# Score matmuls in three fp32r passes over the two row halves, two query tiles started a position ahead, and GpSimd's work of a position tied to VectorE's scalings

## What is computed

```python
q, k, v = split_heads(h, w_qkv, N_HEADS, HEAD_DIM)
q = apply_rope(q, cos, sin) * (HEAD_DIM ** -0.5)
k = apply_rope(k, cos, sin)
oa = moba_attention(q[:, :MOBA_HEADS], k[:, :MOBA_HEADS], v[:, :MOBA_HEADS])
ob = dilated_attention(q[:, MOBA_HEADS:], k[:, MOBA_HEADS:], v[:, MOBA_HEADS:])
o = jnp.concatenate([oa, ob], axis=1)
return merge_heads(o) @ w_o
```

## Time and profile before

| | |
|---|---|
| median of 3 runs (lowest, highest) | 1213.09 us (1212.98, 1213.19) |
| the profiled execution's own time | 1213.26 us |
| its span, first to last instruction | 1211.5 us |
| PE / PEld busy | 1188.8 us (98%) / 1049.2 us (87%) |
| DVE / ACT / POOL busy | 723.8 us (60%) / 628.0 us (52%) / 681.8 us (56%) |
| layer 0's positions 0 to 7 | 75.62 to 234.17 us of the span, 158.55 us |
| PE busy in positions 0 to 5 | all of it |

### The profile page before, as it was taken

One profiled execution on the slowest core, in us unless ns is written; L12 is line 12 of the kernel. 1 busy time (PEld: TensorE's weight loads), 2 busy tenths in 40 slices (PEclk: granted clock), 3 DMA queues, 4 the chain that ended last, 5 costly groups with the idle time before them and its releaser, 6 DMA issues.

```text
span 1211.5 us, 20288 instructions
## 1 busy us (share of the span) xinstructions
PE 1188.8 (98%) x7714; PEld 1049.2 (87%) x7714; DVE 723.8 (60%) x1368; ACT 628.0 (52%) x1089; POOL 681.8 (56%) x418
## 2 busy tenths in 40 slices
PE   9999999899999999999999999999999999999996
PEld 9877777689999999888888788878999999998885
DVE  2045656449988888612280356553999888872126
ACT  3145646446766666622342467663666666662223
POOL 4543535157877777655534332335587777765453
PEclk9999999999999999999999999999999999999999
DMA  7321121221232222432222121112022223233211
GB/s 283 125 72 73 67 85 70 71 105 36 105 112 106 104 106 103 133 130 77 102 105 107 69 71 69 70 70 104 36 106 104 104 104 104 104 133 110 104 69 70
DMA packets 20041, 117.44 MB, mean 97 GB/s; under 512 B 2448, under 2 KB 2832, under 8 KB 7568
## 3 DMA queue, kind: packets, MB, share of 16 engines
q1 hardware_dynamic: 18400, 112.21, 25.8%
q10 hardware_dynamic: 1584, 4.51, 1.1%
HBM read 110.41 MB, written 2.10 MB: 93 GB/s over the span
## 4 chain that ended last, share of the span: by engine, by line
PE 85%; DVE 8%; ACT 2%; POOL 2%; issue 2%; DVEq 0%; ACTq 0%
PE bank L1491 33%; PE bank L1192 29%; PE bank L1223 14%; POOL w_lo L302 2%; PE bank L1275 2%; PE bank L1302 1%; PE bank L1361 1%; PE bank L1340 1%; PE bank L1289 1%; ACT w_hi L403 1%; DVE ln_mul L810 1%; DVE x L833 1%; PE bank L1350 1%; PE bank L1167 1%; DVE x L790 1%
## 5 line engine op out<-in xcount | busy, mean ns | idle before, releaser
L302 POOL TENSOR_TENSOR w_lo<-w_raw,w_hi 128x1024 fp32r<-128x1024 f32 x116 | 299.1, 2600 | 364.4 <-ACT w_hi L403 353.9
L403 ACT ACTIVATE w_hi<-w_raw 128x2048 fp32r<-128x2048 f32 x55 | 105.2, 1912 | 206.1 <-PE bank L1192 197.5
L1491 PE MATMUL bank<-t_hi,w_hi 128*128 128x256 f32 x640 | 181.3, 283 | 2.6 <-DVE w_lo L1046 2.6
L1491 PE MATMUL bank<-t_hi,w_lo 128*128 128x256 f32 x640 | 181.1, 283 | 0.0
L1491 PE MATMUL bank<-t_lo,w_hi 128*128 128x256 f32 x640 | 181.1, 283 | 0.0
L361 POOL TENSOR_TENSOR w_lo<-w_raw,w_hi 128x512 fp32r<-128x512 f32 x120 | 156.1, 1302 | 20.4 <-ACT w_hi L615 19.5
L1192 PE MATMUL bank<-w_hi,a_hi 128*128 128x512 f32 x480 | 153.4, 395 | 3.2 <-POOL w_lo L302 1.8
L1192 PE MATMUL bank<-w_hi,a_lo 128*128 128x512 f32 x480 | 152.0, 391 | 0.0
L1192 PE MATMUL bank<-w_lo,a_hi 128*128 128x512 f32 x480 | 151.8, 391 | 0.0
L1223 PE MATMUL bank<-xt_hi,w_hi 128*128 128x512 f32 (+1 forms) x416 | 147.1, 354 | 2.4 <-ACT v_all L433 1.7
L1223 PE MATMUL bank<-xt_lo,w_hi 128*128 128x512 f32 (+1 forms) x416 | 147.8, 355 | 0.0
(11 more groups left out here) (130 smaller groups left out, 2508.2 us busy)
## 6 DMA issues: line engine op xcount, KB each, us to landing
w_raw<-w_stream SPq DMA_DIRECT2D x97, 1024.0 KB, 4.8
x<-x_in SPq DMA_DIRECT2D x4, 512.0 KB, 7.5
gain<-ln_in ACTq DMA_DIRECT2D x4, 512.0 KB, 5.8
shift<-ln_in ACTq DMA_DIRECT2D x4, 512.0 KB, 7.1
qs<-qc SPq DMA_DIRECT2D x16, 128.0 KB, 2.0
ks<-kc SPq DMA_DIRECT2D x16, 128.0 KB, 2.0
out<-x SPq DMA_DIRECT2D x3, 512.0 KB, 2.6
w_raw<-w_stream SPq DMA_DIRECT2D x2, 512.0 KB, 6.4
```

Source lines behind the costliest of these rows:

```text
L302: pool.tensor_tensor(w_lo[slot(c)][:, part], w_raw[s][:, part], w_hi[slot(c)][:, part].bitcast(F32), ALU.subtract).then_inc(lo_ready, 1)
L403: act.activation(w_hi[slot(c)][:, :], w_raw[c % 2][:, :], ACT.Copy).then_inc(hi_ready, 2)
L1491: mm = pe.matmul(out, lhs[s][:, at], rhs[:, k, :], start=(k, v) == (0, 0), stop=(k, v) == (3, 2))
```

## The change

The scores are computed from split operands. The rotated q and k go to `qa_raw` and `ka_raw`; ScalarE makes their fp32r high parts (`q_heads`, `k_heads`), GpSimd the low part of q (`q_rest`), VectorE that of k (`k_rest`). `scores` then issues for a tile three passes, each with one matmul per head over all its keys (128, 256, 384 or 512 columns). Tiles 0 and 1 lie side by side in a bank, and their scores are issued at the end of the position before; their transposes go together, as do the weighings of tiles 0 and 1 and those of tiles 2 and 3, each value block meeting both query tiles in one matmul. Four places to fill are left of six.

On GpSimd the two units of a chunk's rest are taken apart. The work of a position is in this order: after VectorE's scaling of tile 1 (`p_ok`) the second unit of one chunk and the first product of q; after that of tile 2 the rest of q's rotation, the values' copy and `q_rest`; after `k_ok` the first unit of the next chunk. On ScalarE the weights' heads run one chunk earlier and behind the copy of k; q is copied for two positions ahead at the end of a position. The gain and shift of the first layer norm are loaded after position 7 instead of at the start, since `qa_raw` and `ka_raw` lie in their place.

```diff
-            def rest(c, it=0):
+            def rest(c, it=0, units=(0, 1)):
                 s = c % 2
-                for u in range(2):
+                for u in units:
 
                     pool.wait_ge(hi_ready, 2 * (whole(c) + 2 * it) + u + 1)
                     part = slice(u * UNIT, (u + 1) * UNIT)
                     pool.tensor_tensor(w_lo[slot(c)][:, part], w_raw[s][:, part],
                                        w_hi[slot(c)][:, part].bitcast(F32), ALU.subtract).then_inc(lo_ready, 1)
...
+            def q_cos(i):
 
                 a = A[0]
                 pool.wait_ge(a["q_sw"], 32 * (i + 1))
-                for n, (t, tab) in enumerate(((qc, 0), (qs, 1))):
-                    pool.tensor_tensor(t[:, :], t[:, :], rope[:, tab, :], ALU.mult).then_inc(a["q_m"], 1)
-                pool.wait_ge(a["q_m"], 2 * i + 2)
-                pool.tensor_tensor(qa[slot][:, :], qc[:, :], qs[:, :], ALU.add).then_inc(a["q_ok"], 1)
-                pool.wait_ge(a["q_ok"], i + 1)
+                pool.tensor_tensor(qc[:, :], qc[:, :], rope[:, 0, :], ALU.mult).then_inc(a["q_m"], 1)
+
+            def q_sum(slot, i):
+
+                a = A[0]
+                pool.tensor_tensor(qs[:, :], qs[:, :], rope[:, 1, :], ALU.mult).then_inc(a["q_m"], 1)
+                pool.wait_ge(a["q_m"], 4 * i + 2)
+                pool.tensor_tensor(qa_raw[slot][:, :], qc[:, :], qs[:, :], ALU.add).then_inc(a["q_m"], 1)
+
+            def q_rest(slot, i):
+
+                a = A[0]
+                pool.wait_ge(a["q_m"], 4 * i + 4)
+                pool.tensor_tensor(qa_lo[slot][:, :], qa_raw[slot][:, :], qa_hi[slot][:, :].bitcast(F32),
+                                   ALU.subtract).then_inc(a["q_ok"], 1)
...
+                def even_position(j, it=0):
+
+                    a, i = A[0], 2 * it + j
+                    n, after = (j + 1) % 2, i + 1
+                    pool.wait_ge(a["p_ok"], 4 * i + 2)
+                    rest(b + AT_QK + 2 + j, it, (1,))
+                    q_cos(after)
+                    pool.wait_ge(a["p_ok"], 4 * i + 3)
+                    q_sum(n, after)
+                    take_values(j + 1, it)
+                    q_rest(n, after)
+                    pool.wait_ge(a["k_ok"], after + 1)
+                    rest(b + AT_QK + 3 + j, it, (0,))
...
+            def query_copied(i):
+                a = A[0]
+                act.wait_ge(a["q_mm"], i + 1)
+                act.activation(qc[:, :], bank[0][:, :], ACT.Copy, scale=-MOBA_SCALE).then_inc(a["q_cp"], 1)
+
+            def q_heads(s, i):
+                a = A[0]
+                act.wait_ge(a["q_m"], 4 * i + 3)
+                act.activation(qa_hi[s][:, :], qa_raw[s][:, :], ACT.Copy).then_inc(a["q_m"], 1)
+
+            def k_heads(s, i):
+                a = A[0]
+                act.wait_ge(a["k_m"], 4 * i + 3)
+                act.activation(ka_hi[s][:, :], ka_raw[s][:, :], ACT.Copy).then_inc(a["k_m"], 1)
...
+                exps(0)
+                exps(1)
+                divide(0)
+                divide(1)
+                if before:
+                    out_heads(a, i - 1, (c - 1) % 2)
+                turned(0)
+                exps(2)
+                divide(2)
+                if dense:
+                    act.wait_ge(w_used, b + AT_QK + i + 2)
+                    act.activation(kc[:, :], bank[1][:, :], ACT.Copy).then_inc(a["k_cp"], 1)
+                    heads(b + AT_QK + c + 3, it)
+                exps(3)
+                turned(1)
+                divide(3)
+                if dense:
+                    q_heads((c + 1) % 2, i + 1)
+                turned(2)
+                if dense:
+                    k_heads((c + 1) % 2, i + 1)
+                if early:
+                    query_copied(i + 2)
...
+            def k_rest(a, s, i):
+
+                dve.wait_ge(a["k_m"], 4 * i + 4)
+                dve.tensor_tensor(ka_lo[s][:, :], ka_raw[s][:, :], ka_hi[s][:, :].bitcast(F32),
+                                  ALU.subtract).then_inc(a["k_ok"], 1)
...
+                bounds(0)
+                bounds(1)
+                divide(0)
+                divide(1)
+                turned(0)
+                bounds(2)
+                divide(2)
+                if before:
+                    out_rests(a, i - 1, (c - 1) % 2)
+                turned(1)
+                bounds(3)
                 if dense:
                     rope_k_cos(a, (c + 1) % 2, i + 1)
+                divide(3)
+                if dense:
                     rope_k_sin(a, (c + 1) % 2, i + 1)
-                turn_out(a, NT - 1, 0, 4, 4 * i + NT - 1)
+                turned(2)
+                if dense:
...
-                share = (8, 8, 9, 9, 9, 3) if early else (8, 8, 8, 3, 3) if dense else (3, 5, 7, 7, 6)
+                share = (15, 13, 13, 7) if early else (15, 9, 3, 3) if dense else (9, 9, 7, 5)
...
+                def scores(*tiles, p=par):
+
+                    for qi in tiles:
+                        at, L = P if qi == 1 else 0, (qi + 1) * P
+                        for n, (q, k) in enumerate(((qa_hi, ka_hi), (qa_hi, ka_lo), (qa_lo, ka_hi))):
+                            for h in range(2):
+                                part = slice(64 * h, 64 * h + 64)
+                                mm = pe.matmul(bank[2 + h][:, at:at + L], q[p][part, qi * P:(qi + 1) * P],
+                                               k[p][part, 0:L], start=n == 0, stop=n == 2)
+                    mm.then_inc(a["s_mm"], 1)
...
+                def weigh(*tiles):
+
+                    if tiles[0] == 0:
+                        pe.wait_ge(a["v_pos"], i + 1)
+                    pe.wait_ge(a["tev_v"], 3 * i + max(tiles[-1], 1))
+                    pe.wait_ge(a["tev_a"], 3 * i + max(tiles[-1], 1))
+                    for k in range(tiles[-1] + 1):
+                        q = slice(max(k, tiles[0]) * P, (tiles[-1] + 1) * P)
...
+                            mm = pe.matmul(bank[6 + par][part, q], v_pos[par][:, k, part], probs_t[h][:, k, q],
+                                           start=k == 0, stop=k == tiles[-1])
+                    if tiles[-1] == NT - 1:
                         mm.then_inc(a["pv"], 1)
...
-                pe.wait_ge(a["q_ok"], i + 1)
-                pe.wait_ge(a["k_ok"], i + 1)
-                scores(0)
+                if first:
+                    pe.wait_ge(a["q_ok"], i + 1)
+                    pe.wait_ge(a["k_ok"], i + 1)
+                    scores(0, 1)
                 fill(0)
-                for qi in range(NT):
-                    if qi >= 2:
-                        weigh(qi - 2)
-                    if qi + 1 < NT:
-                        pe.wait_ge(a["s_rd"], 8 * i + 2 * qi + 2)
-                        scores(qi + 1)
-                    fill(qi + 1)
-                    turn(qi)
-                weigh(NT - 2)
-                fill(NT + 1)
-                weigh(NT - 1)
+                turn(0, 0, 1)
+                scores(2)
+                fill(1)
+                turn(1, 2)
+                scores(3)
+                weigh(0, 1)
+                fill(2)
+                turn(2, 3)
+                fill(3)
+                weigh(2, 3)
+                if dense:
+                    pe.wait_ge(a["q_ok"], i + 2)
+                    pe.wait_ge(a["k_ok"], i + 2)
+                    scores(0, 1, p=1 - par)
                 for _ in more:
...
-                    beside = [(0, 0, 0)], [(0, 0, 1), (3, 0, 0), (0, 1), (3, 1, 0)]
+                    beside = [(0, 0, 0)], [(0, 0, 1), (0, 1), (3, 0, 0), (3, 1, 0)]```

Three places in the order of instructions. On PE, in a position of the loop, the second block of transposes and what follows it; before, with tiles 1, 0 and 3:

```order
L1289 MATMUL bank<-ident,probs 128x128 [waits a0_tev_v,a0_tev_a,a0_p_ok1,a0_p_ok]
L1289 MATMUL bank<-ident,probs 128x128 x3
L1302 MATMUL bank<-probs_t,v_pos 64x128 [waits a0_tev_a,a0_tev_v,a0_v_pos]
L1302 MATMUL bank<-probs_t,v_pos 64x128
L1317 REGISTER_ALU
L1275 MATMUL bank<-ka,qa 128x128 [waits a0_s_rd]
L1275 MATMUL bank<-ka,qa 128x128 x7
L1223 MATMUL bank<-xt_lo,w_hi 128x512
```

More of the change, by code:

```diff
@@ L107, in build @@
             qs_raw = [sb(f"qs_raw{s}", [P, 2, Q], stack=st) for s in range(2)]
+        with ExitStack() as st:
+            qa_lo = [sb(f"qa_lo{s}", [P, S], F32R, stack=st) for s in range(2)]
+            ka_lo = [sb(f"ka_lo{s}", [P, S], F32R, stack=st) for s in range(2)]
+        with ExitStack() as st:
+            qa_raw = [sb(f"qa_raw{s}", [P, S], stack=st) for s in range(2)]
+            ka_raw = [sb(f"ka_raw{s}", [P, S], stack=st) for s in range(2)]
         gain = sb("gain", [P, D])
@@ L119, in build @@
             probs_t = [sb(f"probs_t{h}", [P, NT, S], stack=st) for h in range(2)]
+            with ExitStack() as ev:
+                qa_hi = [sb(f"qa_hi{s}", [P, S], F32R, stack=ev) for s in range(2)]
+                ka_hi = [sb(f"ka_hi{s}", [P, S], F32R, stack=ev) for s in range(2)]
             qa = [sb(f"qa{s}", [P, S], stack=st) for s in range(2)]
```

(17 more changed lines are left out.)

157 lines of the change are left out of this document (71 added, 86 removed).

## The result

The changed kernel takes 1203.36 us (median of four runs, 1203.19 to 1203.59), the kernel before 1213.03 beside it: a ratio of 0.9921, 95% interval 0.9904 to 0.9938. The profiled execution took 1203.59 us, its span is 1201.8.

What follows compares the result with a forecast made beforehand. PE's own stream was taken to bound positions 0 to 5, the softmax chain positions 6 and 7. Savings of 9.0 and 0.4 less 0.9 lost, 8.5 us from 1213.09, gave 1204.5 us, range 1201.5 to 1209.5.

Steps and rivals of the forecast that it cites:

- Changes of the array's mode: PE's stream: each change between whole-array, 64-row and 64-column matmuls costs 0.18 us; seven fewer save 1.26 us a position.
- The score passes: Scores in three fp32r passes, heads side by side: 1.91 us a position instead of 2.24.
- either bound: Tile 0's 128-column fp32r pass: 0.065 us as lower bound, 0.224 as upper, 0.112 taken.
- Waits in a steady position: Positions 0 to 5: fills cover the chains to transposes, by 0.03 us at tiles 0 and 1; tile 2 waits 0.1.
- the second rival: Chain to the transposes longer than summed: 0.3 us more costs 4.9 in all, 1209.4 us; chance 0.15.
- q and k for the next pair: Position's end: PE needs them at 18 us, `k_rest` ends at 16.6, a cover of 1.4 us.
- GpSimd: Its units and products keep clear of VectorE's scalings; PE asks for either unit more than 6 us later.
- The term of the sum, 0.9 lost: Position 7: 14.73 us and waits of 1.35, 1.05 and 1.1, so 18.2 us for 17.32, 0.9 lost.
- Position 6: 14.73 us of PE work and waits of 1.0, 2.05 and 0.25: 18.0 us for 18.42, 0.4 saved.
- The sum: Whole kernel: 9.0 us saved in positions 0 to 5, 0.4 in 6, 0.9 lost in 7; 8.5 together, 1204.5 us.

Runs made afterwards that it cites:

- the split weighing: Changed kernel with the fills behind the weighing of tiles 0 and 1 in positions 0 to 5 split four, four, five around its matmuls: 1206.62 us.
- Without GpSimd's places: Changed kernel without GpSimd's waits for the scaling of tiles 1 and 2 and for the next k, one wait for the previous weighing instead: 1207.59 us.
- the last unit held back: Changed kernel with GpSimd's last unit for the output weights waiting for the scaling of tile 1 in position 7: 1202.74 us.
- shares 15, 14, 13, 6: Changed kernel with GpSimd's last unit waiting and one fill of positions 0 to 5 moved from the last place to ahead of tile 2's transposes: 1201.03 us.
- the two runs without them: Changed kernel with PE waiting for copies before scalings ahead of transposes (1204.01 us), and with the last unit waiting and fills 15, 14, 13, 6 (1201.03 us).

## Why the prediction was right, step by step

**Changes of the array's mode**: right. 0.18 was read off as a remainder; the split weighing measures 0.186 directly. The seven fewer make 1.30 us of a looped position's 1.53 (20.47 to 18.94), with 0.33 for the score passes beside them and a new wait of some 0.15 against them. The 0.186 is a price for borders of projection and weighing; for those of the scores only the sums speak. The order alone, with scores in fp32, gives 7.60 of the 9.51 us over positions 0 to 5.

**The score passes**: right. 0.11, 0.12, 0.17 and 0.24 us against 0.112, 0.12, 0.175 and 0.23; going back to fp32 costs 0.31 to 0.35 a position, the 0.33 of 2.24 less 1.91. The price of the 128-column pass, which no row of before showed, lay at the fp32 record's and not at either bound.

**Waits in a steady position**: right by accident. At tile 2 I had 0.1 and found 0.14 to 0.17 in positions 1 to 4 alone, but not for my reason: in the straight positions the same chain fits. Ahead of the first transposes I had 0.31 us too little room. Where PE waits for it, in position 7 with the last unit held back, it is 3.20 us from the first fill's start (207.38 to 210.58) and not 3.42; and 15 fills take 3.54 with the change ahead of them, not 3.45. The error cost nothing in the sum, but it hid that there was room, and it made the second rival likelier than it was.

**q and k for the next pair**: right. `k_rest` ends 1.33 us ahead of the scores that need it (167.83 + 0.69 to 169.85), for a cover of 1.4. Without GpSimd's places this cover goes, as the wait for L970 shows.

**GpSimd**: right in positions 0 to 6. What failed is position 7, where I said that both units come long before PE asks for them, and did not ask what VectorE does meanwhile. The two units run back to back into tile 0's scaling; by the profile's count PE waits 2.09 us for it, and 0.85 where the unit is held back; counted from the end of the last fill's 0.23 us, as in the forecast, 2.24 and 1.01, where I had 1.35. Held back, position 7 takes 17.50 us (206.50 to 224.00) instead of 18.70, where I had 18.2. The term of the sum, 0.9 lost, still measures 0.92, and that is luck: the position is 0.5 longer than I had it, and I had not counted the two matmuls (0.46) that before stood behind its end. The Trainium skill, "SBUF — State Buffer", section on the two separate sides, says that VectorE and GpSimd lock their shared port pair for a whole instruction; the trace agrees, 2.15 us for a scaling of 0.29. I had quoted it and looked only at the places with a wait.

**Position 6**: 17.50 us, not 18.0. Its two waits:

```profile
197.45 0.84 PE L1401 MATMUL bank<-ident,probs 128*128 128x128 f32 x6 [0.64 <-DVE probs L1008]
...
202.57 1.07 PE L1401 MATMUL bank<-ident,probs 128*128 128x128 f32 x8 [1.70 <-ACT probs L524]
```

PE waits 2.4 us in it (17.50 less 15.08 busy). At tiles 2 and 3 that is 0.64 and 1.70 by the profile's count, 0.80 and 1.86 as the forecast counts, which had 1.0 and 2.05. From the matmul behind the scores to the transposes it is 2.97 us (194.48 to 197.45) and 3.46 (199.11 to 202.57), for 3.13 and 3.73. With the 0.22 of the first tiles, the chains that PE waits for were all sized too long, by 0.16 to 0.27.

**The sum.** The 9.7 us are 9.51 in positions 0 to 5, 0.92 in position 6, -0.92 in position 7, and 0.2 outside the eight positions (0.33 less at the start, 0.14 more behind), which no step explains. The forecast had 9.0, 0.4 and -0.9; that is 8.5, and from 1213.09 gives 1204.6, not the 1204.5 written. Of the 1.2 us between 1204.6 and 1203.36, about 0.5 are the waits of position 6 and 0.2 stand outside. The other 0.5 are not chains: without waits a position takes 18.74 us (position 5; with shares 15, 14, 13, 6 all six), where the prices add up to 18.87, 0.8 over six positions. The waits at tile 2 take 0.3 of it back: the two runs without them gained 0.78 and 0.86 us in positions 0 to 5, where I had 0.6. Which of the prices was too high, no run separates.
